# Output projection with the rows in four tiles: which tiles are summed while the weights arrive, and where the transposes stand

## The chip, the core and the metric

The kernel runs on one core of a Trainium2 chip. The core has a matrix engine (TensorE, PE in the profile, with its weight loads as PEld), a vector engine (VectorE, DVE), an activation engine (ScalarE, ACT), GpSimd (POOL) and SyncE (SP), which here only issues DMAs. Each engine takes its own instructions strictly in order and waits on semaphores for the others. Matmul results go to PSUM, which here is eight banks of 128 x 512 numbers; everything else is in SBUF. The metric is the time of the whole kernel on the device in microseconds (us), the median of several executions.

## The reference

Two transformer blocks are computed one after the other on 512 rows of 1024 numbers. Each mixes two branches and then projects the mixture:

```
merged = gate_a * (o_a @ w_branch_a) + gate_b * (o_b @ w_branch_b)      # block 1
y  = merged @ w_out                       # the out projection, 512x1024 @ 1024x1024
x  = x + rmsnorm(y, ln_mix_post)
h2 = rmsnorm(x, ln_mlp_pre)               # goes into a feed-forward layer of width 4096
...
x  = x + (g_a * y_a + g_b * y_b) @ w_out_2                              # block 2
h  = rmsnorm(x, norm2_g)                  # goes into a router and 32 experts
```

rmsnorm divides each row by the root of its mean square and multiplies by a gain. In block 1 the projected rows are normed before they are added to x, in block 2 they are not.

## The kernel before, in words

The kernel is a chain of phases. Each phase has its own semaphores and ends in a barrier of all engines (`Phase.__exit__`, L194 to L196), and no instruction of the next phase starts before it. The change touches `out_phase` (L1550), which runs twice: as "o1" in block 1, followed by the feed-forward phase, and as "o2" in block 2, followed by the router.

Numbers are multiplied as two parts. A float32 matrix is split into a rounded high part (a copy by ACT) and a low part (the difference, by POOL for weights and by DVE for the mixture), and `products` issues three matmuls, high by high, low by high and high by low (L667 to L669). The 1024 inputs are eight slices of 128, counted by k. A weight slice (128 x 1024) is copied by ACT (L1657), its difference is taken by POOL (L1693, semaphore `w_l`); the mixture's slice is copied by ACT (L1658), its difference is taken by DVE (L1740, `m_l`).

The 512 rows are four tiles t of 128 rows, and the 1024 output columns are two halves, so each tile owns two PSUM banks, 2t and 2t+1. `step(k, t, half)` is three matmuls of 128 x 512 into one bank. TensorE's order before: for each k, as its weights come, the four steps of tiles 0 and 1; then, with all weights there, all of tile 2; then `turn(0)` and `turn(1)`; then all of tile 3; then `turn(2)` and `turn(3)`. A turn waits for the normed rows of a tile (`h_ready`) and transposes them in eight 128 x 128 pieces (L345) into the tile's own two banks, four pieces to a bank. `done` counts the finished banks.

The other engines work behind it in an order that is written out by hand and that the change does not touch.

- o1, ACT: squares of a tile's two banks (L1636) and the root of their mean (L1641) for tiles 0 and 1; squares and root of the new x rows (L1645, L1647) for tiles 0 and 1; the high part of the first feed-forward weights (L1677, semaphore `up_h`); L1636 and L1641 for tile 2; the copies of the turned tiles 0 and 1 (`take`, L1653); L1645 and L1647 for tile 2; L1636 and L1641 for tile 3; copies of tile 2; L1645 and L1647 for tile 3; copies of tile 3.
- o1, DVE: sum of the two half-row sums (`mean`, L1704), reciprocal (L1709), multiply by the gain (L1713), add to x (L1717), norm (L1728, L1730, `h_ready`) and the low part of the turned rows (L1736), in the order mean 0, residual 0, mean 1, residual 1, normed 0 and 1, mean 2, residual 2, take 0 and 1, normed 2, mean 3, residual 3, take 2, normed 3, take 3.
- o1, POOL: after the weights, one instruction of 128 x 2048 (L1696), the low part of the first feed-forward weights, as soon as ACT's L1677 is done.
- o2, ACT: L1645 and L1647 for tiles 0 and 1, copies of the turned tile 0 (L1653), L1645 and L1647 for tile 2, copies of tile 1, L1645 and L1647 for tile 3, copies of tiles 2 and 3. DVE: add to x (L1723) for tiles 0 and 1, norm (L1728, L1730) 0 and 1, add 2, norm 2, add 3, norm 3. SP writes every normed tile to memory (L1596) and waits until all four are there.

Of the kernel before, what the change touches and what calls it, by code (L numbers as in the profile page):

```python
# [32 lines left out]
NT = T // P  # L33
D = 1024
KT = D // P
# [304 lines left out]
def turn_rows(pe, banks, rows, ident, turned):  # L340

    for half in range(2):
        for k in range(4):
            c0 = (4 * half + k) * P
            ins = pe.transpose(banks[half][:, k * P:(k + 1) * P], rows[:, c0:c0 + P], ident)  # L345
        ins.then_inc(turned, 1)
# [312 lines left out]
def products(pe, bank, left, right, pairs, start=True, stop=True):  # L659

    for n, (l, r) in enumerate(pairs):
        pe.matmul(bank, left(0, l), right(0, r), start=(start and n == 0), stop=False)  # L667
        pe.matmul(bank, left(0, l), right(1, r), start=False, stop=False)  # L668
        ins = pe.matmul(bank, left(1, l), right(0, r), start=False, stop=(stop and n == len(pairs) - 1))  # L669
    return ins  # L670
# [876 lines left out]
def out_phase(nc, G, name, w_out, rows, gain, ms, branch_gain=None, parts=None, first_up=None, rows_dram=None):  # L1547
# [3 lines left out]
    with Phase(nc, name, "w_h w_l m_h m_l done bsq mean broot gain_in x_ready xsq xroot h_ready turned parted up_in up_h up_l "  # L1551
               "rows_out chain") as ph:
        s = ph.s
# [18 lines left out]
        @block.sync  # L1572
        def _(sp):
            def load(k):
                if k < 2:
                    sp.sem_inc(w_ready[k], 16)
                    return
                if k >= 4:
                    sp.wait_ge(s.w_l, k - 3)
                sp.dma_start(wr[:, OUT_ROOM[k % 4], :], w_out[k * P:(k + 1) * P, :]).then_inc(w_ready[k % 4], 16)  # L1580

            for k in range(KT):
                load(k)
            if branch_gain is not None:
                sp.wait_ge(s.m_l, KT)
                sp.dma_start(gains[0], bcast_rows(branch_gain, 1, D)).then_inc(s.gain_in, 16)
            sp.dma_start(gains[1], bcast_rows(gain, 1, D)).then_inc(s.gain_in, 16)
            for t in range(NT):
                sp.wait_ge(s.w_l, OUT_ROOM.index(t) + 5)
                sp.dma_start(G.X[:, t, :], rows[t * P:(t + 1) * P, :]).then_inc(x_in[t], 16)  # L1590
            if first_up is not None:
                sp.dma_start(first_up[0][:], first_up[1]).then_inc(s.up_in, 16)
            if rows_dram is not None:
                for t in range(NT):
                    sp.wait_ge(s.h_ready, t + 1)
                    sp.dma_start(rows_dram[t * P:(t + 1) * P, :], h[:, t, :]).then_inc(s.rows_out, 16)  # L1596
                sp.wait_ge(s.rows_out, 16 * NT)

        @block.tensor
        def _(pe):  # L1600
            def step(k, t, half):
                return products(pe, bank[2 * t + half][:, :], lambda part, k: ms[:, k, part, t * P:(t + 1) * P],
                                lambda part, k: ws[:, k, part, half * 512:(half + 1) * 512], [(k, k)],
                                start=(k == 0), stop=(k == KT - 1))

            def turn(t):
                pe.wait_ge(s.h_ready, t + 1)
                turn_rows(pe, bank[2 * t:2 * t + 2], h[:, t, :], G.c("ident"), s.turned)

            for k in range(KT):  # L1610
                pe.wait_ge(s.m_l, k + 1)
                pe.wait_ge(s.w_l, k + 1)
                for t in range(2):
                    for half in range(2):
                        ins = step(k, t, half)
                        if k == KT - 1:
                            ins.then_inc(s.done, 1)
            for t in range(2, NT):
                for half in range(2):
                    for k in range(KT):  # L1620
                        ins = step(k, t, half)
                    ins.then_inc(s.done, 1)
                if t == 2:
                    turn(0)
                    turn(1)
            turn(2)
            turn(3)

        @block.scalar
        def _(act):  # L1630
# [2124 lines left out]
```

## Time and profile before

| | us |
|---|---|
| median of 3 executions | 2625.03 (2622.63 to 2628.09) |
| the profiled execution, its own time | 2619.55 |
| its span in the profile | 2617.3 |
| TensorE busy | 2266.3 |
| first to last 128 x 512 matmul of o1 | 961.6 to 1008.7 |
| first matmul of the feed-forward phase after it | 1020.7 |
| first to last 128 x 512 matmul of o2 | 2165.1 to 2212.8 |
| first DMA of the router phase after it | 2220.2 |

The times of single instructions below come from the one profiled execution; they are microseconds from the start of its span. Its own time is 5.48 us below the median. A matmul row's duration contains the overlap with its neighbour: 128 x 512 matmuls start every 0.227 us at the full TensorE clock (2.4 GHz, granted clock 1.0) and every 0.427 us at half of it (1.2 GHz, 0.5).

### The profile page before, as it was taken

The numbers are of one execution on the slowest core, as the hardware profiler recorded it, in microseconds if no ns is written. First come the engines' busy times: TensorE is split into PE (matmuls) and PEld (weight loads), VectorE is DVE, ScalarE is ACT, GpSimd is POOL, SyncE is SP. The second block draws the span as 40 slices with busy tenths as digits, with TensorE's granted clock in tenths as the row PEclk, the third lists the DMA queues.
The fourth block names the chain that finished last, engine by engine and source line by source line (L and its number), as shares of the span: only waits on it lengthen the run. The fifth ranks groups of instructions, "written<-read, shape, count | busy, mean of one in ns | idle before, by whom it ended". The sixth has DMA issues, their size and how long they took to land. (4 is left out here: it accounts for less than half of the span.)

```text
span 2617.3 us, 30359 instructions
## 1 busy us (share of the span) xinstructions
PE 2266.3 (87%) x11615; PEld 1762.5 (67%) x11615; DVE 1094.8 (42%) x1749; ACT 761.1 (29%) x1195; POOL 884.0 (34%) x789
## 2 busy tenths in 40 slices
PE   6999878888868998999996988799997997399994
PEld 4888757777656877788884655688885886344442
DVE  3122356766743145433345554365664435301112
ACT  4333233333314224222214444222122223011110
POOL 3333156565524452444421102334432533000001
PEclk8999889989979998999997999799998998599998
DMA  5323023222114413333314312111101423779994
GB/s 168 89 73 83 18 80 86 73 55 60 46 23 105 113 57 129 113 96 96 96 48 92 65 46 77 29 29 25 21 9 48 118 65 123 295 283 418 419 418 190
DMA packets 284280, 292.95 MB, mean 112 GB/s; under 512 B 77712, under 2 KB 247952, under 8 KB 274512
## 3 DMA queue, kind: packets, MB, share of 16 engines
q1 hardware_dynamic: 272056, 240.58, 29.8%
q10 hardware_dynamic: 6816, 31.46, 2.9%
q0 software_dynamic: 5280, 19.18, 2.1%
q8 instruction: 84, 1.38, 0.2%
q14 instruction: 44, 0.36, 0.0%
HBM read 318.33 MB, written 23.17 MB: 130 GB/s over the span
## 5 line engine op out<-in xcount | busy, mean ns | idle before, releaser
L2244 PE MATMUL moe_bank<-ex_wgu,Y 128*64 128x512 f32 x768 | 172.2, 600 | 3.5 <-DMA ex_wgu<-in_w_up_e 1.9
L667 PE MATMUL gdn_bank<-hh,gdn_ws 128*128 128x512 f32 x256 | 118.7, 464 | 31.1 <-ACT gdn_rn L1165 23.9
L2244 PEld LDWEIGHTS moe_bank<-ex_wgu,Y 128*64 128x64 f32 x768 | 66.2, 139 | 104.1 <-issue 104.1
L2216 POOL DMA_INDIRECT hT<-token_rows,rows x24 | 22.8, 951 | 336.0 <-PE moe_bank L2229 233.1
L667 PE MATMUL m_bank<-hh,m_wgs 128*128 128x512 f32 x256 | 101.4, 396 | 18.1 <-POOL m_wgs L1449 18.1
L1449 POOL TENSOR_TENSOR m_wgs<-hT,m_wgs 128x1024 fp32r<-128x1024 f32 x32 | 80.7, 2526 | 92.3 <-ACT m_wgs L1488 92.2
L1542 DVE TENSOR_TENSOR X<-X,m_bank 128x512 f32<-128x512 f32 x32 | 22.0, 687 | 207.5 <-PE m_bank L669 207.5
L846 POOL TENSOR_TENSOR gdn_ws<-gdn_wr,gdn_ws 128x1024 fp32r<-128x1024 f32 x30 | 71.2, 2374 | 110.0 <-ACT gdn_ws L1116 110.0
L668 PE MATMUL gdn_bank<-hl,gdn_ws 128*128 128x512 f32 x256 | 105.6, 413 | 0.0
L667 PE MATMUL ff_bank<-ff_wds,ff_hes 128*128 128x512 f32 x256 | 100.7, 393 | 4.9 <-DVE Y L1932 4.9
L669 PE MATMUL gdn_bank<-hh,gdn_ws 128*128 128x512 f32 x256 | 104.9, 410 | 0.0
L1932 DVE TENSOR_TENSOR Y<-Y,ff_bank 128x512 f32<-128x512 f32 x128 | 84.3, 684 | 47.0 <-PE ff_bank L669 47.0
L668 PE MATMUL m_bank<-hl,m_wgs 128*128 128x512 f32 x256 | 100.9, 394 | 0.0
L669 PE MATMUL m_bank<-hh,m_wgs 128*128 128x512 f32 x256 | 100.6, 393 | 0.0
L668 PE MATMUL ff_bank<-ff_wds,ff_hes 128*128 128x512 f32 x256 | 100.4, 392 | 0.0
L669 PE MATMUL ff_bank<-ff_wds,ff_hes 128*128 128x512 f32 x256 | 100.3, 392 | 0.0
L1922 DVE TENSOR_TENSOR hT<-hT 128x512 f32<-128x512 f32 x32 | 37.0, 1159 | 149.6 <-ACT hT L1885 149.6
L1820 POOL TENSOR_TENSOR ff_wds<-ff_wd,ff_wds 128x2048 fp32r<-128x2048 f32 x16 | 74.5, 4654 | 69.9 <-ACT ff_wds L1878 69.9
L2267 PE MATMUL moe_bank<-ex_wd,hT 128*64 128x512 f32 x384 | 87.7, 597 | 6.6 <-DVE hT L2336 6.5
L420 POOL TENSOR_TENSOR att_wqk<-Y,att_wqk 128x1024 fp32r<-128x1024 f32 x24 | 58.0, 2421 | 100.0 <-ACT att_wqk L523 100.0
L667 PE MATMUL att_bank<-att_hh,att_wqk 128*128 128x512 f32 x192 | 79.2, 412 | 13.1 <-POOL att_wqk L420 7.0
L2330 DVE TENSOR_TENSOR hT<-hT,moe_bank 128x256 f32<-128x256 f32 x24 | 10.1, 421 | 174.6 <-ACT hT L2298 174.6
(568 smaller groups left out, 6145.5 us busy)
## 6 DMA issues: line engine op xcount, KB each, us to landing
ex_wgu<-in_w_gate_e SPq DMA_DIRECT2D x42, 1024.0 KB, 16.9
ex_wgu<-in_w_up_e SPq DMA_DIRECT2D x42, 1024.0 KB, 19.8
ex_wd<-in_w_down_e SPq DMA_DIRECT2D x42, 1024.0 KB, 22.1
Y<-in_w_in SPq DMA_DIRECT2D x48, 512.0 KB, 4.0
hT<-in_w_in SPq DMA_DIRECT2D x34, 512.0 KB, 4.2
wu<-in_w_ff SPq DMA_DIRECT2D x16, 1024.0 KB, 11.8
ff_wd<-in_w_ff SPq DMA_DIRECT2D x16, 1024.0 KB
gdn_wr<-in_w_in SPq DMA_DIRECT2D x30, 512.0 KB, 4.0
```

The costliest lines, as they stand in the source:

```text
L420: pool.tensor_tensor(wqk[:, n % 2, 1], wr[:, r % 2], wqk[:, n % 2, 0], ALU.subtract).then_inc(s.lo, 1)
L667: pe.matmul(bank, left(0, l), right(0, r), start=(start and n == 0), stop=False)
L668: pe.matmul(bank, left(0, l), right(1, r), start=False, stop=False)
L669: ins = pe.matmul(bank, left(1, l), right(0, r), start=False, stop=(stop and n == len(pairs) - 1))
L846: pool.tensor_tensor(ws[:, r % 2, 1], raw[r], ws[:, r % 2, 0], ALU.subtract).then_inc(s.lo, 1)
L1449: pool.tensor_tensor(wgs[:, r % 3, 1], wg[n], wgs[:, r % 3, 0], ALU.subtract).then_inc(s.gate_l, 1)
L1820: pool.tensor_tensor(wds[:, j, 1], wd[:], wds[:, j, 0], ALU.subtract).then_inc(s.down_l, 1)
L1922: dve.tensor_tensor(he[:, f, :], rl[:, f, :], rl[:, f, :], ALU.mult).then_inc(s.square, 1)
L1932: dve.tensor_tensor(y, y, bank[4 + o % 4][:, :], ALU.add).then_inc(s.added, 1)
L2216: pool.indirect_dma_start(hg[:, j, :], None, rows_dram, bass.IndirectOffsetOnAxis(rows[:, pair_of[q]:pair_of[q] + 1], 0)).then_inc(h_in[j] ...
L2244: ins = pe.matmul(bank[2 + j][half, :], hgT[:, j, k, half], w[:, e, k], start=(k == 0), stop=(k == KT - 1))
L2267: ins = pe.matmul(bank[5 + half][r, :], heT[:, j, f, r], wd[:, b, e, f, half * 512:(half + 1) * 512], start=(f == 0), stop=(f == 1))
```

## The change

While the weights come, TensorE now does the steps of three tiles for each k, where it did two. Tile 3 follows as before once all weights are there. The four turns stand together behind the last product; before, those of tiles 0 and 1 stood between tile 2 and tile 3. Both executions of `out_phase` are changed alike, and no other engine's code.

```diff
             for k in range(KT):
                 pe.wait_ge(s.m_l, k + 1)
                 pe.wait_ge(s.w_l, k + 1)
-                for t in range(2):
+                for t in range(3):
                     for half in range(2):
                         ins = step(k, t, half)
                         if k == KT - 1:
                             ins.then_inc(s.done, 1)
-            for t in range(2, NT):
-                for half in range(2):
-                    for k in range(KT):
-                        ins = step(k, t, half)
-                    ins.then_inc(s.done, 1)
-                if t == 2:
-                    turn(0)
-                    turn(1)
-            turn(2)
-            turn(3)
+            for half in range(2):
+                for k in range(KT):
+                    ins = step(k, 3, half)
+                ins.then_inc(s.done, 1)
+            for t in range(NT):
+                turn(t)
```

TensorE at the start of o1's products, before: the end of weight slice 0 and the start of slice 1. `o1_bank2` and `o1_bank3` are the two halves of tile 1, `o1_bank0` is the first half of tile 0.

```order
L667 MATMUL o1_bank2<-o1_ws,split1 128x512
L668 MATMUL o1_bank2<-o1_ws,split1 128x512
L669 MATMUL o1_bank2<-o1_ws,split1 128x512
L667 MATMUL o1_bank3<-o1_ws,split1 128x512
L668 MATMUL o1_bank3<-o1_ws,split1 128x512
L669 MATMUL o1_bank3<-o1_ws,split1 128x512
L667 MATMUL o1_bank0<-o1_ws,split1 128x512
```

The same place on TensorE in the changed kernel. `o1_bank4` and `o1_bank5` are the halves of tile 2.

```order
L667 MATMUL o1_bank3<-o1_ws,split1 128x512
L668 MATMUL o1_bank3<-o1_ws,split1 128x512
L669 MATMUL o1_bank3<-o1_ws,split1 128x512
L667 MATMUL o1_bank4<-o1_ws,split1 128x512
L668 MATMUL o1_bank4<-o1_ws,split1 128x512
L669 MATMUL o1_bank4<-o1_ws,split1 128x512
L667 MATMUL o1_bank5<-o1_ws,split1 128x512
L668 MATMUL o1_bank5<-o1_ws,split1 128x512
L669 MATMUL o1_bank5<-o1_ws,split1 128x512
L667 MATMUL o1_bank0<-o1_ws,split1 128x512
```

Six matmuls of tile 2 have moved in front of the next slice's first matmul, in each of the eight slices.

TensorE at the end of tile 2 in o1, before: the last product of tile 2, the turns of tiles 0 and 1 (banks 0 to 3), and the first products of tile 3 (bank 6).

```order
L669 MATMUL o1_bank5<-o1_ws,split1 128x512
L345 MATMUL o1_bank0<-const,hT 128x128 x4
L345 MATMUL o1_bank1<-const,hT 128x128 x4
L345 MATMUL o1_bank2<-const,hT 128x128 x4
L345 MATMUL o1_bank3<-const,hT 128x128 x4
L667 MATMUL o1_bank6<-o1_ws,split1 128x512
L668 MATMUL o1_bank6<-o1_ws,split1 128x512
```

The same turns in the changed kernel, behind the last product of tile 3 (bank 7):

```order
L668 MATMUL o1_bank7<-o1_ws,split1 128x512
L669 MATMUL o1_bank7<-o1_ws,split1 128x512
L345 MATMUL o1_bank0<-const,hT 128x128 x4
L345 MATMUL o1_bank1<-const,hT 128x128 x4
L345 MATMUL o1_bank2<-const,hT 128x128 x4
L345 MATMUL o1_bank3<-const,hT 128x128 x4
L345 MATMUL o1_bank4<-const,hT 128x128 x4
```

Sixteen transposes have moved behind the 48 matmuls of tile 3. In o2 the order changes in the same way.

## Rows read from the trace of the kernel before

**Rows 1.** The page: busy time by engine, its share of the span, instructions.
```profile
PE 2266.3 (87%) x11615; PEld 1762.5 (67%) x11615; DVE 1094.8 (42%) x1749; ACT 761.1 (29%) x1195; POOL 884.0 (34%) x789
```

**Rows 2.** Windows over the products of o1 and of o2.
```profile
core 0: us, PE busy (x) PEld busy (x) DVE busy (x) ACT busy (x) POOL busy (x), PEclk, DMA share, GB/s
961.50:1008.60 47.10, 47.02 (x208) 38.76 (x208) 37.06 (x32) 23.56 (x44) 23.74 (x8) 0.97 0.41 137
2165.10:2212.70 47.60, 47.58 (x209) 39.35 (x210) 28.50 (x20) 16.19 (x26) 19.05 (x7) 0.95 0.40 133
```

**Rows 3.** Timeline of o1, POOL and TensorE: start, duration, engine, line, names, count, idle before.
```profile
958.62 22.01 POOL L1693 TENSOR_TENSOR o_ws<-X,o_ws 128x1024 fp32r<-128x1024 f32 x8 [20.39 <-ACT o_ws L1657]
961.58 0.80 PE L667 MATMUL o_bank<-o_ws,split 128*128 128x512 f32 x1 [6.48 <-DVE split L1740]
982.68 0.39 PE L669 MATMUL o_bank<-o_ws,split 128*128 128x512 f32 x1
995.60 0.39 PE L669 MATMUL o_bank<-o_ws,split 128*128 128x512 f32 x1
995.83 1.91 PE L345 MATMUL o_bank<-const,hT 128*128 128x128 f32 x16
997.50 0.47 PE L667 MATMUL o_bank<-o_ws,split 128*128 128x512 f32 x1
1016.33 1.97 PE L345 MATMUL o_bank<-const,hT 128*128 128x128 f32 x8 [5.23 <-DVE hT L1730]
```

**Rows 4.** Timeline of o1, ACT, DVE and POOL.
```profile
983.17 0.60 ACT L1636 ACTIVATE Y<-o_bank 128x512 f32<-128x512 f32 x1 [8.56 <-PE o_bank L669]
987.20 1.41 DVE L1713 SCALAR_TENSOR_TENSOR Y<-o_bank,o_ss,Y 128x512 f32<-128x512 f32 x2 [0.92 <-DMA Y<-in_ln_mlp_pre]
994.38 0.29 ACT L1647 ACTIVATE o_ss<-o_ss,eps 128x1 f32<-128x1 f32 x1
996.33 1.91 ACT L1677 ACTIVATE split<-wu 128x2048 fp32r<-128x2048 f32 x1 [1.65 <-DMA wu<-in_w_ff]
998.32 4.61 POOL L1696 TENSOR_TENSOR split<-wu,split 128x2048 fp32r<-128x2048 f32 x1 [17.69 <-ACT split L1677]
999.43 3.52 DVE L1704 TENSOR_TENSOR o_ss<-o_ss 128x1 f32<-128x1 f32 x1 [3.23 <-ACT Y L1636]
1002.98 0.29 ACT L1641 ACTIVATE o_ss<-o_ss,eps 128x1 f32<-128x1 f32 x1 [3.58 <-DVE o_ss L1704]
1009.87 0.15 DVE L1704 TENSOR_TENSOR o_ss<-o_ss 128x1 f32<-128x1 f32 x1
1010.06 0.29 ACT L1641 ACTIVATE o_ss<-o_ss,eps 128x1 f32<-128x1 f32 x1 [0.67 <-DVE o_ss L1704]
1018.97 0.69 DVE L1736 TENSOR_TENSOR hl<-o_bank,hh 128x512 fp32r<-128x512 f32 x1 [0.16 <-ACT hh L1653]
```

**Rows 5.** Timeline of o2, TensorE, ACT, DVE and SP.
```profile
2200.03 1.91 PE L345 MATMUL o_bank<-const,Y 128*128 128x128 f32 x16
2200.66 1.09 ACT L1653 ACTIVATE hT<-o_bank 128x512 f32<-128x512 f32 x2 [7.83 <-PE o_bank L345]
2201.63 1.06 ACT L1645 ACTIVATE Y<-X 128x1024 f32<-128x1024 f32 x1
2202.81 0.29 ACT L1647 ACTIVATE o_ss<-o_ss,eps 128x1 f32<-128x1 f32 x1
2203.34 1.28 DVE L1730 SCALAR_TENSOR_TENSOR Y<-X,o_ss,o_gain 128x1024 f32<-128x1024 f32 x1
2212.68 1.03 PE L345 MATMUL o_bank<-const,Y 128*128 128x128 f32 x8
2212.88 0.69 DVE L1723 TENSOR_TENSOR X<-X,o_bank 128x512 f32<-128x512 f32 x1 [4.70 <-PE o_bank L669]
2213.60 1.06 ACT L1645 ACTIVATE Y<-X 128x1024 f32<-128x1024 f32 x1 [9.52 <-DVE X L1723]
2216.65 1.27 PE L345 MATMUL o_bank<-const,Y 128*128 128x128 f32 x8 [2.93 <-DVE Y L1730]
```

## The prediction

> **What bounds the kernel now.** I read the page first: TensorE is busy 87% of the span and no other engine half of it [rows 1]. That share says little about this change, which takes no matmul away. What counts is which wait ends each of the two phases concerned, so I went on to the windows, and then to the timelines engine by engine.
>
> The windows say that both stretches of products are full: TensorE is busy 47.02 of 47.10 us in o1 and 47.58 of 47.60 in o2 [rows 2]. So the products are not short of weights. The timeline says the same: POOL hands over eight slices in 22.01 us, one every 2.75 us from 958.62 on, and the last stands at 980.63 [rows 3]. TensorE needs 12 x 0.227 = 2.72 us for a slice with two tiles and starts late and at half clock, so it reaches the last slice after 84 matmuls, at 982.68 - 2 x 0.227 = 982.2 (the row at 982.68 is the 87th matmul, the last of tile 0's first bank). It is always a little behind its supply. More work for each slice therefore fills no hole, because there is none.
>
> What ends each phase is the work behind the products. In o1 the last product stops at about 1008.5 (the window is full to 1008.6, rows 2), but the last subtraction of DVE at 1019.66 [rows 4], and the feed-forward phase comes after. In that tail TensorE waits for DVE (5.23 us before the last turn, rows 3). DVE is set back by its own earlier order: the mean of tile 3 runs at 1009.87, with the root behind it at 1010.06 [rows 4]; from tile 2's root at 1002.98 on, DVE works through tile 2 without a hole that matters. So o1's end hangs on tile 2's root, not on the last product. In o2 it hangs on the last product: DVE adds tile 3's second half at 2212.88 after waiting for TensorE, ACT squares it at 2213.60, and norm, turn and the write to memory follow [rows 5].
>
> **The change, part by part.** *Products.* A matmul starts every (995.60 - 982.68) / 57 = 0.227 us [rows 3]. Tile 0's first bank was finished after 87 matmuls; now two more steps precede it in each of seven slices, 42 matmuls, so it is finished 42 x 0.227 = 9.5 us later, and all banks of tiles 0 and 1 with it. Tile 2's first bank is 21 matmuls later, its second is finished at the same place in the stream (144th). Tile 3 comes sooner by the 16 transposes that no longer cut the stream: 997.50 - 995.83 = 1.67 us [rows 3]. No wait is added in the loop: a slice takes 18 x 0.227 = 4.1 us and one arrives every 2.75.
>
> *o1.* The chain of tiles 0 and 1 starts at 983.17 + 9.5 = 992.7. It gets 0.9 us back, the wait for the gains' DMA before the multiply at 987.20, because that DMA does not wait for TensorE [rows 4]. So everything up to tile 1's second root shifts by 8.6: that root goes from 994.38 to 1003.0. Behind it stands ACT's copy of the feed-forward weights. Before, it waited 1.65 us for its DMA and started at 996.33; now the DMA has long landed and it starts when the root's 0.29 us are over, at 1003.0 + 0.29 = 1003.3. Shift 6.9 us. POOL's subtraction follows at once, 998.32 + 6.9 = 1005.2 to 1009.8 (4.61 us). ACT's squares of tile 2 follow the copy, so they shift by 6.9 too.
>
> Now comes the price of the whole thing. DVE's mean of tile 2, one number per partition, took 3.52 us where the mean of tile 3 took 0.15; it began at 999.43 while POOL's subtraction ran and ended at 1002.95, 0.02 us after it [rows 4]. DVE stood still for POOL. All of the participants shift by the same 6.9 us, POOL still starts 1.1 us before the mean, so I expect the same stall, and tile 2's root at 1002.98 + 6.9 = 1009.9. Without the stall the mean would run at 1006.3 and the root at 1006.5, 3.5 later than before. I take 6.9, the one row that there is.
>
> The Trainium skill (SBUF — State Buffer, "Who interferes with whom") says that a VectorE instruction with two SBUF inputs and a GpSimd instruction that reads SBUF exclude each other, and that the one which started later waits for the whole of the other. The mean has two SBUF inputs and the trace agrees with its 3.52 us; by this rule the shift is 6.9, by mere sharing of bandwidth a number per partition would cost nearly nothing and it is 3.5.
>
> Before, this stall lay beside tile 3's matmuls, which ran to 1008.5, and tile 3's part on DVE then followed tile 2's. Now the last product is done at 1008.5 - 1.7 = 1006.8, before tile 2's root even starts. The turns of tiles 0 and 1 follow at 1006.8 and are read by ACT after that root, so they hold up nothing. From the root on it is the old chain, all in order of DVE: o1 ends 6.9 us later. The 1.7 us won on TensorE go into idle time.
>
> *o2.* There is no mean, no POOL work and no weight copy in the tail. Tiles 0 and 1 are 9.5 us later. They were normed by 2200.03, when they were turned, so they are by 2209.5, and nobody needs them before the turns, which come later still. But ACT's order has the copy of turned tile 0 in front of tile 2's squares. The turn of tile 0 was at 2200.03; now it is at 2212.68 - 1.66 = 2211.0. From there on by the old distances [rows 5]: copy after 0.63 (2211.65), squares of tile 2 after 0.97 (2212.6), root after 1.18 (2213.8), norm after 0.53 (2214.3), for 1.28 (2215.6). Only then comes DVE to adding tile 3, which is finished since 2211.0: two halves of 0.69 each (2217.0), squares at 2217.0 instead of 2213.60. Shift 3.4 us, and behind it norm, turn, copy and memory write as before. What was hidden beside tile 3's matmuls, a copy, squares, root and norm of tile 2, is now in the open; only 1.7 us come back for it.
>
> *Clock.* Eight transposes took 1.03 us in one row and 1.97 in another [rows 5, 3], the second after 5.23 us idle, at half clock. Now tile 2's turn also stands behind an idle stretch (6 us or more in o1, 3 in o2), and tile 3's in o2 too. In o1 it is 0.9 us on something that ACT does not wait for at that point; in o2's last turn 1.97 - 1.27 = 0.7 at most, beside the write to memory, which starts at the same moment. I count 0, with 0.7 as the upper bound and nothing below.
>
> The Trainium skill (TensorE: Matmul & The Clock Gate, "Why this matters for your kernels") warns that idle gaps between matmul bursts bring TensorE back to half rate. The 1.97 us row agrees; by it the upper bound of 0.7 would be the value, and the sum 11.0 instead of 10.3.
>
> *Sum.* 6.9 + 3.4 = 10.3 us. Each phase starts behind a barrier, and the next phase's first DMAs and matmuls with it, so I carry the shifts to the end undiminished. The profiled execution's 2619.55 becomes 2629.9. It lies 5.5 us under the median of the runs, so for the median I expect 2625.03 + 10.3 = 2635.3.
>
> **Rivals.** *DVE is not held by POOL this time.* Then o1 costs 3.5, in all 6.9: 2631.9. For it: there is one such row only. Against it: it ended within 0.03 us of POOL's, and nothing in the meeting changes.
>
> *TensorE sets the end after all.* In each phase the 16 transposes leave the stream, 1.67 + 1.66 = 3.3 us, and if the end moves with the last product the time is 2621.7, faster. It decides from the point where tile 2's root in o1 stands by 1002.98 - 1.67 = 1001.3, and where in o2 ACT has tile 2's squares done without the copy of tile 0 before them. Against it: the root can't come before 1006.5 even without the stall, and the order on ACT is fixed. Only if I misread who waits for whom does it hold.
>
> *It is absorbed later.* If the next phases waited for something with its own clock, the shift would vanish, 2625. Against: their DMAs are issued after the barrier.
>
> *Half clock lasts longer.* After a longer idle the first 24 matmuls of the feed-forward phase could stay at 0.427 us for as many again: 24 x 0.2 = 4.8 us more, 2640.1. For it: 12 us of nearly idle TensorE become 20. Against: the granted clock is already at its lower level there.
>
> **How the numbers follow.** My forecast 0.68, no hold by POOL 0.12, longer half clock 0.10, absorbed 0.06, TensorE sets the end 0.04. A change under 0.2%, 5.2 us, can't be told from none in this kernel. Absorbed counts as same; of the case without the hold (+6.9) about half falls there by scatter, as does a little of the forecast; the last case is faster by less than 0.2% most of the time. That gives slower 0.82, same 0.15, faster 0.03. The three executions differ by 3 us either way from their median; so the range runs from 2631.9 less 3 to 2635.3 + 0.7 with 4 for scatter and part of the clock case: 2629 to 2640.
>
> **What would show it.** In the changed profile the tail of o1 (last 128 x 512 matmul to first of the feed-forward phase) should grow from 12.2 to about 20.8 us (12.2 + 1.7 + 6.9), with the mean of tile 2 again 3 to 4 us long and ending with POOL's L1696; the first squares of o1 should be 9.5 us later from the phase's first matmul. In o2 ACT should idle before the copy of turned tile 0 for some 9 us (7.83 before), and DVE should add tile 3 right behind tile 2's norm. If the mean takes 0.15 us, the first rival is right; if the tail of o1 stays near 12 us, the forecast is wrong, and if the phases stretch as said but the whole does not, the sum's last step is.

## The result, and the profile after

| | before | changed |
|---|---|---|
| median of 6 executions each | 2625.82 us (2622.63 to 2629.03) | 2639.02 us (2633.66 to 2641.54) |
| profiled execution, its own time | 2619.55 | 2640.47 |
| span in the profile | 2617.3 | 2638.5 |

The changed kernel is slower: ratio 1.0047, 95% interval 1.0036 to 1.0058, which is 13.2 us by the medians and 9.5 to 15.2 us by the interval. The forecast was 2635.3 us, 10.3 us more than before, with a range of 2629 to 2640; the measured median lies 1.0 us under the upper end of it.

The two profiles differ by 21.2 us, twice the forecast. Before any cause is sought in them, the span has to be cut at the phases. The cuts are the first weight copy of o1 and the first matmul behind it, and the first weight copy of o2 and the first DMA behind it. First the rows of the kernel before (timeline: start, duration, engine, line, names, count, idle before):

```profile
957.49 1.06 ACT L1657 ACTIVATE o_ws<-X 128x1024 fp32r<-128x1024 f32 x1 [9.91 <-SPq L1576]
1020.69 0.77 PE L667 MATMUL ff_bank<-hh,split 128*128 128x512 f32 x1 [2.39 <-ACTq L1865]
2161.03 1.06 ACT L1657 ACTIVATE o_ws<-X 128x1024 fp32r<-128x1024 f32 x1 [7.10 <-SPq L1576]
2220.20 0.38 SPq L1994 DMA_DIRECT2D Y<-in_w_router  x1
```

The same four in the changed kernel, whose lines behind TensorE's part stand four lower:

```profile
964.58 1.06 ACT L1653 ACTIVATE o_ws<-X 128x1024 fp32r<-128x1024 f32 x1 [9.91 <-SPq L1576]
1034.83 0.77 PE L667 MATMUL ff_bank<-hh,split 128*128 128x512 f32 x1 [2.39 <-ACTq L1861]
2178.52 1.06 ACT L1653 ACTIVATE o_ws<-X 128x1024 fp32r<-128x1024 f32 x1 [7.10 <-SPq L1576]
2240.94 0.38 SPq L1990 DMA_DIRECT2D Y<-in_w_router  x1
```

By subtraction, o1 went from 63.20 to 70.25 us (+7.05) and o2 from 59.17 to 62.42 (+3.25). That is 10.30 us. The other 10.9 us of difference between these two profiles lie where nothing was changed: 7.09 us ahead of o1, 3.35 between the phases, 0.46 behind o2. The experiments below make it likely that this is scatter from execution to execution. From here on I read o1 and o2 from their own beginnings.

Windows over the changed kernel: products of o1, its tail, products of o2, its tail.

```profile
core 0: us, PE busy (x) PEld busy (x) DVE busy (x) ACT busy (x) POOL busy (x), PEclk, DMA share, GB/s
968.60:1013.90 45.30, 45.23 (x192) 37.31 (x193) 28.61 (x23) 19.17 (x34) 20.52 (x8) 0.96 0.42 141
1013.90:1034.80 20.90, 5.96 (x34) 4.83 (x33) 16.62 (x22) 8.97 (x20) 3.16 (x1) 0.65 0.00 0
2182.60:2228.40 45.80, 45.79 (x192) 37.70 (x193) 26.18 (x17) 12.82 (x19) 19.05 (x7) 0.95 0.38 127
2228.40:2241.00 12.60, 5.09 (x34) 4.12 (x32) 4.10 (x7) 7.00 (x14) 0.00 (x0) 0.77 0.20 83
```

The products are still without a hole, now with the 192 products alone. The edges of these windows are rounded, so the two stretches are measured from the start of the first product to the start of the last: in o1 46.69 us before (961.58 to 1008.27) and 45.11 in the changed kernel (968.67 to 1013.78), in o2 47.32 (2165.12 to 2212.44) and 45.68 (2182.61 to 2228.29). Each is 1.6 us shorter. TensorE did get faster at what was changed. What grew are the tails.

The chain of o1 in the changed kernel, on ACT, DVE, POOL and TensorE, to be held against [rows 3, 4]:

```profile
999.99 0.60 ACT L1632 ACTIVATE Y<-o_bank 128x512 f32<-128x512 f32 x1 [18.41 <-PE o_bank L669]
1010.33 0.29 ACT L1643 ACTIVATE o_ss<-o_ss,eps 128x1 f32<-128x1 f32 x1
1010.53 1.91 ACT L1673 ACTIVATE split<-wu 128x2048 fp32r<-128x2048 f32 x1
1012.51 4.55 POOL L1692 TENSOR_TENSOR split<-wu,split 128x2048 fp32r<-128x2048 f32 x1 [24.78 <-ACT split L1673]
1013.61 3.47 DVE L1700 TENSOR_TENSOR o_ss<-o_ss 128x1 f32<-128x1 f32 x1 [1.48 <-ACT Y L1632]
1014.01 1.91 PE L345 MATMUL o_bank<-const,hT 128*128 128x128 f32 x16
1017.11 0.29 ACT L1637 ACTIVATE o_ss<-o_ss,eps 128x1 f32<-128x1 f32 x1 [3.53 <-DVE o_ss L1700]
1024.14 1.97 PE L345 MATMUL o_bank<-const,hT 128*128 128x128 f32 x8 [8.22 <-DVE hT L1726]
1033.10 0.69 DVE L1732 TENSOR_TENSOR hl<-o_bank,hh 128x512 fp32r<-128x512 f32 x1 [0.16 <-ACT hh L1649]
```

The mean (L1700) begins 1.1 us after POOL's subtraction and ends within 0.02 us of it, as before. But the last product starts at 1013.78, only 0.2 us after the mean, and the sixteen transposes follow at 1014.01. Beside nearly the whole stall there is now nothing on TensorE but turns that nobody reads yet.

The chain of o2 in the changed kernel, to be held against [rows 5]. The first line is DVE's adding of tile 2:

```profile
2221.42 1.28 DVE L1719 TENSOR_TENSOR X<-X,o_bank 128x512 f32<-128x512 f32 x2
2228.52 1.91 PE L345 MATMUL o_bank<-const,Y 128*128 128x128 f32 x16
2229.15 1.09 ACT L1649 ACTIVATE hT<-o_bank 128x512 f32<-128x512 f32 x2 [9.19 <-PE o_bank L345]
2230.12 1.06 ACT L1641 ACTIVATE Y<-X 128x1024 f32<-128x1024 f32 x1
2231.83 1.28 DVE L1726 SCALAR_TENSOR_TENSOR Y<-X,o_ss,o_gain 128x1024 f32<-128x1024 f32 x1
2233.03 1.28 DVE L1719 TENSOR_TENSOR X<-X,o_bank 128x512 f32<-128x512 f32 x2
2234.34 1.06 ACT L1641 ACTIVATE Y<-X 128x1024 f32<-128x1024 f32 x1 [1.77 <-DVE X L1719]
2236.05 1.28 DVE L1726 SCALAR_TENSOR_TENSOR Y<-X,o_ss,o_gain 128x1024 f32<-128x1024 f32 x1
2237.39 1.97 PE L345 MATMUL o_bank<-const,Y 128*128 128x128 f32 x8 [3.13 <-DVE Y L1726]
```

ACT stands idle for 9.19 us in front of the copy of turned tile 0. For the last 6.4 of them tile 2's rows are ready for its squares (2221.42 + 1.28 = 2222.70), and everything of tile 2 comes behind the copy.

### The profile page after: what moved, and what is told of

It reads as the page before. It is cut to its first block and busy times, and to the rows that moved or that the text cites. A ratio compares the mean times of both kernels' runs of the same rounds, so it can differ in the third digit from the quotient of the medians.

```text
span 2638.5 us, 30359 instructions
## 1 busy us (share of the span) xinstructions
PE 2284.8 (87%) x11615; PEld 1778.3 (67%) x11615; DVE 1096.4 (42%) x1749; ACT 761.8 (29%) x1195; POOL 883.3 (33%) x789
## 5 line engine op out<-in xcount | busy, mean ns | idle before, releaser
L667 PEld LDWEIGHTS gdn_bank<-hh,gdn_ws 128*128 128x128 f32 x256 | 52.6, 205 | 47.2 <-issue 27.9
```

## The experiments

Each profile was cut in the same five parts (us):

| | ahead of o1 | o1 | between | o2 | behind |
|---|---|---|---|---|---|
| before | 957.49 | 63.20 | 1140.34 | 59.17 | 397.10 |
| before, again | 960.17 | 63.23 | 1143.73 | 59.40 | 398.17 |
| changed | 964.58 | 70.25 | 1143.69 | 62.42 | 397.56 |
| changed, again | 961.40 | 70.09 | 1143.45 | 62.45 | 397.51 |
| change in o1 alone | 964.20 | 70.30 | 1143.54 | 59.40 | 397.96 |
| change in o2 alone | 961.69 | 63.27 | 1137.02 | 62.29 | 397.83 |
| turns alone | 957.79 | 65.57 | 1144.84 | 62.32 | 397.38 |
| changed, without POOL's L1692 | 960.50 | 66.80 | 1140.30 | 62.30 | 397.70 |
| before, without POOL's L1696 | 960.66 | 62.89 | 1143.95 | 59.34 | 397.16 |
| changed, mean as a reduce | 960.48 | 68.08 | 1142.37 | 62.48 | 397.49 |
| change in o2 with ACT's order changed too, mean as a reduce in o1 | 957.00 | 62.72 | 1140.69 | 57.41 | 397.08 |
| orders fitted in both, mean as a reduce | 962.41 | 61.22 | 1142.35 | 57.41 | 396.91 |

**Is the rest of the difference scatter?** Both kernels were profiled a second time without an edit. Of the kernel before:

> The kernel before, unchanged, profiled once more. Cut the span into five parts: start to the first weight copy of o1, o1 (to the first matmul of the feed-forward phase), the phases between, o2 (first weight copy to the router's first DMA), the rest. In the first pair of profiles the changed kernel was longer by 7.05 us in o1 and 3.25 in o2, but also by 7.09, 3.35 and 0.46 us in parts that the change does not touch. Theory (scatter between executions): o1 is again 63.2 and o2 59.2 us, within 0.3, while the untouched parts move by some us against the first profile (957.5, 1140.3, 397.1). Rival (the changed kernel slows other parts too): the untouched parts repeat the first profile within 1 us.

Of the changed kernel:

> The changed kernel, profiled once more. Theory: o1 is again 70.25 us and o2 62.4 within 0.3, and the parts that the change does not touch (964.6, 1143.7 and 397.6 in its first profile) move within what the other profiles show: 957.0 to 964.6, 1137.0 to 1144.8, 397.1 to 398.2. Rival (the change slows the part ahead of o1 too, which was 7.1 us longer than in the first profile of before): that part is again at 964 or more.

The second profile of before has o1 and o2 within 0.03 and 0.23 us of the first, while its unchanged parts are 7.1 us longer. The second of the changed kernel has them within 0.16 and 0.03, and the part ahead of o1 at 961.40, not at 964 or more. Held against each other, the two second profiles (spans 2624.7 and 2634.9) differ by 10.2 us: 6.86 in o1, 3.05 in o2, 0.29 elsewhere.

So the part ahead of o1 is not always slowed, which speaks against the rival. Profiles alone don't exclude it: the unchanged parts have a mean of 2502.5 us in the five profiles with the third tile in o1's loop and of 2498.8 in the other seven, while each of the two groups spreads by 7 us. The medians of the kernels below tell more, since they come from more executions. Four of them contain a part of the change or the change with an edit, and are slower than before by 5.6, 3.3, 5.7 and 8.2 us in their medians, where their cut phases grew by 7.1, 3.1, 5.5 and 8.2 (in the order of the text). A cost outside of o1 and o2 that is clear of the scatter shows in none of them, so it is unlikely.

The unchanged parts add up to between 2494.8 and 2505.8 us over the twelve profiles, and the first profile of before, from which the durations were taken, was one of the shortest. A cut phase repeats to 0.25 us where the whole scatters by ten, so each of the following verdicts is read from the cut.

**Each phase alone.** The edit is shown without the lines that only follow from it:

```diff
-                for t in range(2):
+                for t in range(3 if name == 'o1' else 2):     # 'o2' in the other kernel
...
-                if t == 2:
+                if t == 2 and not (name == 'o1'):
                     turn(0)
                     turn(1)
```

> The change in o1 alone, o2 as before. Theory: o1 is 70.2 us (+7.0), o2 59.2, and the whole is 7 us slower than before, ratio about 1.0027. Rival 1 (both phases share the cost another way): o1 within 1 us of 63.2. Rival 2 (the untouched parts are slowed by the changed o1): the whole is 10 us or more slower.

Measured: o1 70.30, o2 59.40; median 2630.96 us beside 2625.39 of before, ratio 1.0021 (1.0009 to 1.0033).

> The change in o2 alone, o1 as before. Theory: o2 is 62.4 us (+3.3), o1 63.2, and the whole is 3.3 us slower, ratio about 1.0013, hardly to be told from none. Rival (untouched parts are slowed too): 6 us or more slower.

Measured: o2 62.29, o1 63.27; median 2628.71 beside 2625.39, ratio 1.0016 (1.0005 to 1.0027). Each phase keeps its cost when the other is as before, and the costs of 7.1 and 3.1 us add up to the 10.3 of the cut. The two intervals contain the forecast ratios (1.0027 and 1.0013); they would also contain others, so the cut decides here.

**The turns alone.** The loop keeps its two tiles; only the turns go to the end. The edit in plain form:

```diff
             for t in range(2, NT):
...
-                if t == 2:
-                    turn(0)
-                    turn(1)
-            turn(2)
-            turn(3)
+            for t in range(NT):
+                turn(t)
```

> Both phases with two tiles in the loop over the weights as before, but all four turns behind the last product. Theory: in o2 the whole cost is ACT's copy of turned tile 0 standing ahead of tile 2's squares, so the turns alone bring all of it: o2 62.4 us. In o1 the stall of DVE behind POOL stays hidden (tile 2's root at its old distance), only the copies and squares of tile 2 wait for the turns: o1 about 66.1 us (+2.9, worked out by the old distances). Rival (what costs is that tiles 0 and 1 are finished 9.5 us later): o1 and o2 as before or up to 1.7 us shorter, 61.5 and 57.5.

Measured: o2 62.32, o1 65.57; median 2631.10 beside 2625.39, ratio 1.0031 (1.0021 to 1.0041). In o2 the turns bring the whole cost and the third tile in the loop none. In o1 they bring 2.4 us (2.9 was expected) and the third tile the other 4.7. The rows of that kernel on ACT show the wait in o1:

```profile
1003.35 0.29 ACT L1641 ACTIVATE o_ss<-o_ss,eps 128x1 f32<-128x1 f32 x1 [3.58 <-DVE o_ss L1704]
1007.68 2.06 ACT L1653 ACTIVATE hh<-o_bank 128x512 fp32r<-128x512 f32 x4 [4.03 <-PE o_bank L345]
1009.60 1.08 ACT L1645 ACTIVATE hT<-X 128x1024 f32<-128x1024 f32 x1
```

Tile 2's squares in the kernel before:

```profile
1006.20 1.06 ACT L1645 ACTIVATE hT<-X 128x1024 f32<-128x1024 f32 x1 [0.99 <-DVE X L1717]
```

Tile 2's root comes at 1003.35, early as before, but its squares stand behind four copies that wait 4.03 us for TensorE. Counted from o1's beginning the squares are 3.1 us later than before (51.81 against 48.71). Before, the norm behind them had to wait for DVE's subtractions; here these are done by then, and 0.7 us are made up. The expectation of 2.9 did not count this in full.

**Without POOL's subtraction.** The edit is the same in both kernels:

```diff
             if first_up is not None:
                 pool.wait_ge(s.up_h, 1)
-                pool.tensor_tensor(ms[:, :, 1, 0:DE], first_up[0][:], ms[:, :, 0, 0:DE], ALU.subtract)
```

> The changed kernel without POOL's subtraction for the first feed-forward weights (L1696 before, L1692 after); it leaves out the low part of those weights. Theory (tile 2's mean on DVE stands still for POOL, and this stall is in the open now): the mean takes 0.15 us, o1 shrinks from 70.25 us by 3.4 to 66.8. Rival (the mean is long for another reason, a late ACT result for instance): the mean still takes about 3.5 us and o1 stays at 70.2.

> The kernel before without the same subtraction (it leaves out the low part of the first feed-forward weights). Theory (before, the stall lay beside tile 3's matmuls): the mean takes 0.15 us, but o1 shrinks only from 63.2 by 0.4 to 62.8, since tile 3's last product now sets the chain. Rival (the stall counted fully before too, so it adds nothing to the change): o1 shrinks by 3.4 to 59.8.

The mean of tile 2 on DVE, first in the changed kernel without the subtraction, then in the kernel before without it:

```profile
1009.39 0.16 DVE L1699 TENSOR_TENSOR o_ss<-o_ss 128x1 f32<-128x1 f32 x1 [1.47 <-ACT Y L1632]
```

```profile
1002.77 0.16 DVE L1703 TENSOR_TENSOR o_ss<-o_ss 128x1 f32<-128x1 f32 x1 [3.32 <-ACT Y L1636]
```

It takes 0.16 us in both. The changed kernel's o1 falls by 3.45 us to 66.80; that of before by 0.31 to 62.89. Each of the two was executed once (2629.42 and 2625.73 us), so only the cut is read. The same stall of 3.4 us was worth 0.3 before and 3.45 now: this is the loss of cover that the forecast rested on, shown from both sides. It also shows how close the two candidates for o1's end stood before: tile 2's root set it, but without the stall tile 3's last product would have set it only 0.3 us earlier.

**The mean as a reduce.** POOL keeps its work and DVE's instruction changes its form.

```diff
-                dve.tensor_tensor(ss[:, 0, t:t + 1], ss[:, 6, t:t + 1], ss[:, 7, t:t + 1], ALU.add).then_inc(s.mean, 1)
+                dve.tensor_reduce(ss[:, 0, t:t + 1], ss[:, 6:8, t], AX, ALU.add).then_inc(s.mean, 1)
```

> The changed kernel with the mean's sum of two columns as one TENSOR_REDUCE over one tensor instead of a TENSOR_TENSOR of two; POOL's work stays. Theory (DVE waits for POOL where its instruction reads two tensors in SBUF): the reduce takes under 0.3 us, then the add to x of tile 2 (two tensors in SBUF) is the one that waits, until POOL ends, so o1 is 2.1 us shorter than 70.25, about 68.1. Rival (any DVE instruction waits while POOL works): the reduce takes 3.5 us and o1 stays at 70.2.

POOL and DVE of that kernel around tile 2:

```profile
1008.39 4.56 POOL L1692 TENSOR_TENSOR split<-wu,split 128x2048 fp32r<-128x2048 f32 x1 [24.76 <-ACT split L1673]
```

```profile
1009.50 0.16 DVE L1700 TENSOR_REDUCE o_ss<-o_ss 128x1 f32<-128x2 f32 x1 [1.47 <-ACT Y L1632]
1010.02 0.16 DVE L1705 RECIPROCAL o_ss<-o_ss 128x1 f32<-128x1 f32 x1 [0.36 <-ACT o_ss L1637]
1010.22 1.41 DVE L1709 SCALAR_TENSOR_TENSOR Y<-o_bank,o_ss,Y 128x512 f32<-128x512 f32 x2
1011.66 2.37 DVE L1713 TENSOR_TENSOR X<-X,Y 128x1024 f32<-128x1024 f32 x1
```

While POOL works until 1012.95, the reduce, the reciprocal and the multiply (one operand in PSUM) go through at their usual lengths. The add of two SBUF tensors takes 2.37 us where it takes 1.23 otherwise. It ends 1.08 us after POOL, nearly its own length, so it looks as if it waited for POOL's end and then ran; in the same way the one-number mean ended 0.02 us after POOL. o1 is 68.08 us, expected 68.1; the median is 2633.36 beside 2625.20, ratio 1.0033 (1.0016 to 1.0050). The Trainium skill (SBUF — State Buffer, "Who interferes with whom") names just this distinction, two SBUF inputs on VectorE against a GpSimd instruction that reads SBUF, and no contention for a reduce; the rows agree.

**ACT's order in o2.** Three tiles and turns at the end in o2 alone, squares first; o1 as before with the reduce. The edit on ACT:

```diff
-                for t in range(2):
-                    squares(t)
-                for t in range(2, NT):
-                    take(t - 2)
-                    squares(t)
-                take(2)
-                take(3)
+                for t in range(NT):
+                    squares(t)
+                for t in range(NT):
+                    take(t)
```

> o1 as before but for the mean as a reduce; o2 with three tiles in the loop and all turns at the end, and with ACT's order changed: squares and roots of all four tiles first, copies of the turned tiles behind them. Theory: in o2 tile 2's squares no longer wait behind the copy of tile 0, so the 16 transposes saved from the stream show at last: o2 57.5 us (59.2 before, 62.4 with the change). o1 62.8. The whole 2 us faster than before, not to be told from none. Rival (finishing tiles 0 and 1 later costs by itself): o2 stays above 59.2.

ACT at the end of that kernel's o2, with tile 3's squares ahead of all eight copies:

```profile
2211.21 1.06 ACT L1645 ACTIVATE Y<-X 128x1024 f32<-128x1024 f32 x1 [5.22 <-DVE X L1720]
2212.60 3.99 ACT L1653 ACTIVATE hT<-o_bank 128x512 f32<-128x512 f32 x8
```

Measured: o2 57.41, o1 62.72. The median is 2622.72 beside 2625.20, ratio 0.9998 (0.9986 to 1.0009), no difference that the whole time can show. In o2 the same TensorE order that cost 3.2 us now gains 1.8, with nothing else changed than what ACT puts first; the products' stretch is shorter by the same 1.8 (45.56 us instead of 47.32). ACT's new order with TensorE's old one was not run.

**Orders fitted in both phases.** All turns at the end, o2 as in the kernel ahead, two tiles in o1's loop; on ACT and DVE tile 2's squares and norm ahead of the copies of tiles 0 and 1.

```diff
                 branch_root(2)
-                take(0)
-                take(1)
                 squares(2)
                 branch_squares(3)
                 branch_root(3)
-                take(2)
+                take(0)
+                take(1)
                 squares(3)
+                take(2)
                 take(3)
...
                 residual(2)
-                take(0)
-                take(1)
                 normed(2)
                 mean(3)
                 residual(3)
-                take(2)
+                take(0)
                 normed(3)
+                take(1)
+                take(2)
                 take(3)
```

> All turns behind the last product in both phases, and the orders of ACT and DVE fitted to it: in o1 two tiles in the loop, the mean as a reduce, squares and norm of tile 2 ahead of the copies of the turned tiles 0 and 1, which go beside tile 3's chain; o2 as in the last version. Theory (the turns cost only where squares or norms stand behind the copies): with nothing of tile 2 behind a copy, o1 ends with tile 3's own chain, 1.7 us earlier by the transposes saved, less what DVE's remaining subtractions add at the end, about 0.7: o1 61.7 us, o2 57.4, the whole about 3 us faster than before. Rival (o1 is bound by the sum of DVE's work in its tail, not by the order): o1 stays at 62.7 or more.

ACT in o1 of that kernel: tile 2's squares, then the copies of tiles 0 and 1 behind tile 3's root:

```profile
1009.07 1.06 ACT L1645 ACTIVATE hT<-X 128x1024 f32<-128x1024 f32 x1 [4.14 <-DVE X L1714]
1012.99 2.04 ACT L1653 ACTIVATE hh<-o_bank 128x512 fp32r<-128x512 f32 x4
```

Measured: o1 61.22, o2 57.41, together 3.7 us less than before; median 2622.70 beside 2628.00, ratio 0.9984 (0.9971 to 0.9996). This is the only kernel of the study whose interval lies wholly under 1, and only just. The gain of 5.3 us between the medians is not to be read finer than its interval; the cut says 3.7. The rival is out: with all of DVE's work in place, the orders of TensorE, ACT and DVE together made o1 1.5 us shorter than in the kernel ahead of it. Which of the three brings how much was not run apart.

## Why the prediction was right

*Products.* Tile 0's first squares were to come 9.5 us later; from o1's first weight copy they came after 35.41 us instead of 25.68, 9.7 later. The stream of products shrank by 1.58 us in o1 and 1.64 in o2 (1.67 expected).

*o1.* Tile 1's second root shifted by 8.9 us (8.6 forecast), POOL's subtraction by 7.1 (6.9), tile 2's root by 7.04 (6.9), DVE's last subtraction by 7.04, all from o1's beginning. The stall was to be repeated, and was, with 3.47 us; its price in the open was to be 3.4 us and is 3.45. The 0.15 us by which 6.9 falls short of 7.05 come with the first term, which is 0.2 too small here. The forecast took the start of the products as the same in both kernels, but it varies from execution to execution: in the first profile of before the first 7 distances between matmuls of o1 are those of half clock (0.427 us and more), in that of the changed kernel the first 8. In the second pair it is 8 and 7, and the squares come 9.35 us later (35.26 against 25.91). The tail of o1 was to grow by 8.6 us; from the start of the last product to the feed-forward phase's first matmul it grew by 8.6, from 12.42 to 21.05.

*o2.* The copy of tile 0 was to start 50.6 us after the phase's first weight copy, and did (2229.15 - 2178.52 = 50.63). Tile 3's squares shifted by 3.25 us instead of 3.4: two halves of L1719 take 1.28 us together, where I had 0.69 for each; that is 0.1 of the missing 0.15.

*Clock.* Counted at zero with 0.7 as the bound, and zero it was. o2's last turn did take 1.97 us, after 3.13 us idle and at a granted clock of 0.50, and the Trainium skill's warning (TensorE: Matmul & The Clock Gate, "Why this matters for your kernels") holds to that extent; but from the last norm to the router's first DMA it is 4.89 us in both kernels (2215.31 to 2220.20, 2236.05 to 2240.94), so the slower turn is hidden.

*The sum.* 10.3 us were forecast and the cut phases grew by 10.30. That close a hit is luck: o1 grew by 0.15 more than forecast and o2 by 0.15 less, and the second pair of profiles gives 6.86 + 3.05 = 9.9. The medians differ by 13.2, and the forecast's 10.3 lies inside the interval. The remaining 2.9 us have no settled place: outside of o1 and o2 the first pair of profiles differs by 10.9 us and the second by 0.29. I take them for scatter of medians of six; the change in each phase alone made the medians 5.6 and 3.3 us longer, together 8.9 and so on the other side of 10.3. It is likely but not shown, since only single executions were profiled. With the median 1.0 us from the end of the range, a little more of such scatter would have put it outside, with the mechanism unchanged.

*The rivals.* Without the hold by POOL o1 was to cost 3.5 us, and with POOL's work left out it costs 66.80 - 63.20 = 3.6. TensorE as the one that sets the end needs tile 2's squares out of the copies' way; that is the condition which the last two kernels create in o2, and there the end does come earlier by the transposes (1.8 us). In the changed kernel as it is the condition isn't met. Nothing seems absorbed later: the part behind o2 is the same to 0.7 us in both pairs of profiles of the two kernels, and that between the phases is 3.35 us longer in one pair and 0.28 shorter in the other. Half clock in the feed-forward phase did not last as much longer as the rival had it: in the changed kernel's trace its first 14 matmuls take 5.96 us (1034.83 to 1040.79), in that of before 5.84 (1020.69 to 1026.53), so it is 0.1 us and not 4.8. Nor are 24 matmuls at half clock in either trace: the first 12 distances between matmuls are those of half clock before, the first 13 in the changed kernel.

## What to carry to other kernels

Where a busy engine's stream is reordered, its own gain counts for little; ask which short waits of the other engines lay beside the part that was moved, and what in their fixed orders stands behind a copy that now comes later. In this kernel a turn at the end was cheap only where squares and norms of later tiles went ahead of the copies of earlier ones. And when the whole scatters by more than the effect, cut the span at barriers: a phase of 60 us repeated within 0.25 us where the whole moved by ten.

## What the runs showed of the hardware

An instruction of DVE on one number per partition took 3.47 us because POOL was in the middle of a subtraction, and 0.16 us in the same place written as a reduce over one tensor. The reciprocal (0.16 us) and a multiply with one operand in PSUM (two halves in 1.41 us) ran at full speed beside POOL at the same time; the add behind them, with both operands in SBUF, took 2.37 us instead of 1.23. I had expected the stall from one row, but not that the form of so small an instruction would be worth 2.2 us of the phase (70.25 to 68.08).
